# Two-layer hybrid attention trunk on one core: attention steps, weight splits and evictions put in another order inside the projection stages

## What is computed

```
h    = rmsnorm(x, norm_g)
proj = h @ w_in                      # 2048 -> 6400 columns: aq ak av ag bq bk bv bg
ya   = chunk_relbias_attention(...)  # mixer A: 16 heads of 64, own chunk + 8 before, bias by distance
ya   = ya * silu(ag)
yb   = swa_sink_gqa(...)             # mixer B: 16 query heads, 2 key heads, rotary, window 128, sinks
yb   = yb * silu(bg)
x    = x + concat([ya, yb]) @ w_out
```

## Time and profile before

| what | value |
|---|---|
| median of three executions | 1678.8 us |
| the profiled execution, its time | 1680.35 us |
| its span, first to last instruction | 1678.6 us |
| busy: PE, DVE, ACT, POOL | 96%, 76%, 56%, 23% |
| mean granted clock of PE | 0.994 |

### The profile page before, as it was taken

How to read it: one execution, slowest core, us unless ns; L and a number is a source line. 1 busy time by engine, 2 the same in 40 slices (tenths; PEclk the granted TensorE clock), 3 DMA queues, 4 the chain that set the end, 5 groups by cost and what they waited for, 6 DMA issues and landing times.

```text
span 1678.6 us, 28680 instructions
## 1 busy us (share of the span) xinstructions
PE 1613.9 (96%) x9257; PEld 1404.2 (84%) x9257; DVE 1279.6 (76%) x2747; ACT 935.3 (56%) x1969; POOL 386.4 (23%) x554
## 2 busy tenths in 40 slices
PE   8999999999999999999999999999999999999997
PEld 7888888888778888899987888888887888888997
DVE  7777777877677787888877777777776777788875
ACT  7656555565456665533465556655564566664333
POOL 1632332334022210000054332332321221000000
PEclk9999999999999999999999999999999999999999
DMA  6232333223422322344432322333324223233343
GB/s 229 79 94 76 98 97 101 87 81 95 158 91 90 103 97 91 109 157 153 158 112 72 104 90 80 96 94 99 94 80 162 88 93 115 76 113 107 129 142 113
DMA packets 77509, 180.67 MB, mean 108 GB/s; under 512 B 9408, under 2 KB 13792, under 8 KB 70640
## 3 DMA queue, kind: packets, MB, share of 16 engines
q1 hardware_dynamic: 76960, 178.99, 32.4%
q10 hardware_dynamic: 432, 0.55, 0.1%
q0 software_dynamic: 32, 0.08, 0.0%
HBM read 163.25 MB, written 11.62 MB: 104 GB/s over the span
## 4 chain that ended last, share of the span: by engine, by line
PE 48%; issue 29%; POOL 15%; DVE 4%; ACT 2%; POOLq 1%; DMA 0%; DVEq 0%; SPq 0%; ACTq 0%
PE ps_proj L711 9%; PE ps_proj L712 9%; PE ps_proj L713 9%; POOL w_raw L2251 4%; POOL w_raw L2253 3%; POOL w_raw L2256 3%; POOL w_raw L2254 3%; DVE w_lo L1553 1%; PE ps_o L993 1%; PE ps_o L997 1%; PE ps_o L998 1%; PE ps_o L823 1%; PE ps_s L798 1%; PE ps_s L982 1%; PE ps_s L981 1%
## 5 line engine op out<-in xcount | busy, mean ns | idle before, releaser
L1092 ACT ACTIVATE w_hi<-w_raw 128x512 fp32r<-128x512 f32 (+1 forms) x528 | 377.9, 726 | 234.2 <-DVE w_raw L1925 56.0
L1553 DVE TENSOR_TENSOR w_lo<-w_raw,w_hi 128x512 fp32r<-128x512 f32 (+1 forms) x528 | 442.3, 848 | 48.8 <-ACT w_hi L1092 45.4
L711 PE MATMUL ps_proj<-act_hi,w_hi 128*128 128x512 f32 x704 | 277.9, 395 | 0.0
L713 PE MATMUL ps_proj<-act_hi,w_lo 128*128 128x512 f32 x704 | 275.9, 392 | 0.0
L712 PE MATMUL ps_proj<-act_lo,w_hi 128*128 128x512 f32 x704 | 275.9, 392 | 0.0
L1553 DVE TENSOR_TENSOR arena<-ps_t,arena 128x512 fp32r<-128x512 f32 (+4 forms) x168 | 85.0, 509 | 130.1 <-ACT arena L1092 129.5
L2251 POOL TENSOR_TENSOR w_raw<-w_raw 128x128 f32<-128x128 f32 x112 | 65.0, 580 | 457.3 <-DMA w_raw<-w 457.3
L713 PEld LDWEIGHTS ps_proj<-act_hi,w_lo 128*128 128x128 f32 x704 | 132.8, 189 | 28.8
L711 PEld LDWEIGHTS ps_proj<-act_hi,w_hi 128*128 128x128 f32 x704 | 133.0, 189 | 25.0
L1158 ACT ACTIVATE probs<-probs,nmax 128x128 f32<-128x128 f32 (+3 forms) x128 | 72.0, 562 | 146.5 <-DVE nmax L1625 146.3
L712 PEld LDWEIGHTS ps_proj<-act_lo,w_hi 128*128 128x128 f32 x704 | 133.1, 189 | 24.4
(11 more groups left out here) (374 smaller groups left out, 4555.8 us busy)
## 6 DMA issues: line engine op xcount, KB each, us to landing
w_raw<-w SPq DMA_DIRECT2D x322, 256.0 KB, 3.0
w_raw<-w SPq DMA_DIRECT2D x51, 1024.0 KB, 4.9
temp<-temp SPq DMA_DIRECT2D x72, 64.0 KB, 4.2
strips_tables<-ext SPq DMA_DIRECT2D x16, 256.0 KB, 3.9
temp<-xT SPq DMA_DIRECT2D x16, 256.0 KB, 4.3
xs<-xy SPq DMA_DIRECT2D x16, 256.0 KB, 4.2
temp<-xs SPq DMA_DIRECT2D x16, 256.0 KB, 4.1
strips_tables<-ext SPq DMA_DIRECT2D x16, 224.0 KB, 4.1
```

Of the source, the lines that this page charges most:

```text
L711: pe.matmul(dst, wh, act_hi[:, k, :], start=start, stop=False)
L713: return pe.matmul(dst, wl, act_hi[:, k, :], start=False, stop=stop)
L1092: return nc.scalar.activation(dst, src, ACT.Copy, scale=scale)
L1553: return nc.vector.tensor_tensor(dst, src, hi, ALU.subtract)
```

## The change

Nothing is computed in another way; steps stand at other places. `values_a` goes from points 7 and 13 to 8 and 14, two points behind the last transposes it needs. ACT's `half_out` goes with it but stands last in its point, and DVE's `sum_halves` goes to points 12 and 15, with `gated` behind the second. ACT's normalising goes from the end of point p to the start of point p + 1. DVE does `lo_in` before `lo_p`, where it was after. DVE's splits of q and k for the next pair: k one point later (ACT's `hi_k` at 12, DVE's `lo_k` at 13). DVE's take of the second half, at a stage's end before, goes behind the first bias, low part and inversion of the next stage; stage 1 leaves it out. In the mixed stage PE no longer waits for a bank before the first two tiles.

```
-PV_A = (7, 13)
+PV_A = (8, 14)
+HALF_OUT_AT = (8, 14)
+SUM_HALVES_AT = (12, 15)
-HI_Q_AT, LO_Q_AT, HI_K_AT, LO_K_AT = 10, 11, 11, 12
+HI_Q_AT, LO_Q_AT, HI_K_AT, LO_K_AT = 10, 11, 12, 13
...
             def unit(T, att):
                 for s in range(4):
-                    wait_bank(T, s)
+                    if s > 1:
+                        wait_bank(T, s)
...
-            def softmax_a(e0, e, other):
-                n = (e % QT + 1) * P
-                row = probs[:, e % 2, 0:n]
+            def exp_a(e0, e):
+                row = probs[:, e % 2, 0:(e % QT + 1) * P]
...
-                other()
+            def normalise_a(e0, e):
+                row = probs[:, e % 2, 0:(e % QT + 1) * P]
                 act.wait_ge(rden_done, e0 + (e + 1))
                 copy(row, row, scale=rden[:, e % 2, 0:1]).then_inc(normed, 1)
...
+                if p - 1 in SCORES_A:
+                    normalise_a(e0, SCORES_A.index(p - 1))
                 if p in TURN_A:
                     hi_p(g, e0, TURN_A.index(p))
-                if p in PV_A:
-                    half_out(g, PV_A.index(p))
                 if p in SCORES_A:
-                    softmax_a(e0, SCORES_A.index(p), other)
-                else:
-                    other()
+                    exp_a(e0, SCORES_A.index(p))
+                other()
+                if p in HALF_OUT_AT:
+                    half_out(g, HALF_OUT_AT.index(p))
...
                 if p in SCORES_A:
                     bias_a(v, L * PAIRS + ab, e0, SCORES_A.index(p))
+                other()
                 if p in TURN_A:
                     lo_p(e0, TURN_A.index(p))
-                if p in PV_A:
-                    h = PV_A.index(p)
+                if p in SCORES_A:
+                    invert(e0, SCORES_A.index(p))
+                if p in SUM_HALVES_AT:
+                    h = SUM_HALVES_AT.index(p)
                     sum_halves(g, h, tile, (L * PAIRS + ab) * 2)
                     if h == 1:
                         gated(g, tile)
-                other()
-                if p in SCORES_A:
-                    invert(e0, SCORES_A.index(p))
...
                     attend(att, p, L, ab, Y_STAGE, other)
+                    if p == 0 and not first:
+                        take_pair(T - 4, L, u - 1, 1, ((t_graw, 0.5), (t_v, 1.0)))
...
-                take_pair(T, L, u, 1, ((t_graw, 0.5), (t_v, 1.0)))
...
                         attend(att, p, L, ab, ab, lambda: split_w(T, s + 1, pt))
+                        if p == 0:
+                            take_pair(T - 4, L, PAIRS - 1, 1, ((t_graw, 0.5), (t_v, 1.0)))
```

More of the change, by code:

```diff
@@ L1356, in duties @@
                 if kind == "b":
-                    if p == HI_K_AT:
+                    if p == 11:
                         hi_k(lambda: act.wait_ge(rope_done, L * ROPES + 1))
@@ L1770, in duties @@
                         take(T, 1, t_q)
-                    if p == LO_K_AT:
+                    if p == 12:
                         lo_k(L * V_LAYER + PAIRS)
@@ L1813, in take_pair, with unit_sums @@
                                                    ).then_inc(proj_free, 1)
-            def unit_sums(T, L, u, att, ab, g, v):
+            def unit_sums(T, L, u, att, ab, g, v, first=False, last=False):
                 for p in range(16):
                     def other():
-                        if isinstance(u, int) and p + LO_AHEAD >= 16:
+                        if last and p + LO_AHEAD >= 16:
                             lo_next(tile0(L) + A_SLOTS, p + LO_AHEAD - 16)
@@ L1822, in other @@
                             lo_in(T, p + LO_AHEAD)
-                    if p == PV_A[0]:
+                    if p == SUM_HALVES_AT[0]:
                         dve.wait_ge(y_kept, L * (16 * (PAIRS - 2)) + u * 16)
@@ L2103, in _ @@
                     carry_wait(dve)
-                with dve.Fori(1, PAIRS - 1) as u:
+                unit_sums(T + 4, L, 1, att_a(L, 0), 0, pair_a(L, 1), L * V_LAYER + 1, first=True)
+                with dve.Fori(2, PAIRS - 1) as u:
                     unit_sums(T + u * 4, L, u, att_a(L, u - 1), u - 1, pair_a(L, u), L * V_LAYER + u)
                 u = PAIRS - 1
-                unit_sums(T + u * 4, L, u, att_a(L, u - 1), u - 1, pair_a(L, u), L * V_LAYER + u)
+                unit_sums(T + u * 4, L, u, att_a(L, u - 1), u - 1, pair_a(L, u), L * V_LAYER + u, last=True)
                 unit(T + A_SLOTS, L, att_a(L, PAIRS - 1), PAIRS - 1, ("b", None, None))
```

## The result

The changed kernel takes 1699.17 us (median of four, 1698.0 to 1702.16) against 1678.13 (1676.68 to 1679.56) for the kernel before beside it: a ratio of 1.0128 with an interval of 1.0111 to 1.0146. It is slower; 1672 was predicted, and the range ended at 1691. The profiled execution took 1702.16 with a span of 1700.4, 21.8 more than before. The mean granted clock fell from 0.994 to 0.979.

A forecast was written before the change was run, and what follows sets the result against it. PE, busy 96% of the span, was taken as the bound, so only its waits could be won. 12 x 0.2 - 2 x 1.8 - 2 x 3.1 = -7.4 us gave 1672 us, range 1650 to 1691.

The forecast's parts named there:

- Waits that go: PE's waits before points 1, 10, 13 and 15 vanish in a middle stage; about 0.3 of 0.76 us stays at 12.
- `gated` at t = 1.3: DVE's 13.7 us of work ends `gated` 1.3 us after a stage's first score product (t = 0).
- L = 3.4: Landing time of chunk 4's load behind the store of y: 3.4 us, with bounds 3.0 and 4.7.
- third rival: Slower: load still lands after 4.7, wait 4.1 at point 3, half clock in every stage; 1693 us, chance 0.25.
- The rest of the chain: From chunk 4's landing to point 3 on PE: 2.86 + 1.99 us, plus 0.45 for the low part ahead of `lo_p` 0.
- The wait before point 3: PE waits for chunk 4's chain in stages 2 to 7: 2.8 us, against 0.65 before.
- Three in four of them at 1.65: Half clock behind the point 3 wait in three of four of stages 2 to 7: 1.2 us a stage.
- Stages 2 to 7, +0.2 each: Twelve stages each end 0.2 us longer: waits win 1.0, half clock costs 1.2.
- Stage 1: No store ahead of its chunk 4 in SP's list; small waits go, winning about 1.8 us, twice.
- The mixed stage, -3.1 each: Bank wait and half clock behind it go, less 0.4 at the first bias and 0.4 at point 3; 3.1 us won, twice.
- some 0.4 more at point 3 for the reordered `lo_p`: Mixed stage: low part now ahead of `lo_p` adds some 0.4 us of wait at point 3.
- Normalising costs nothing: ACT's normalising moved to the next point's start costs nothing of its own; uncovered it would be 0.5 to 0.7 us.

The follow-up runs named there:

- before_y_late: Kernel before the change, with the store of y moved behind the next stage's loads of chunks 4 and 5: 1677.07 us, ratio 0.9983.
- fill: Changed kernel with twelve unread 512-column products on PE before point 3 in stages 2 to 7: 1680.48 us, ratio 1.0014.
- take_end: Changed kernel with the second half's take back at the stage's end and the mixed stage's bank waits back: 1684.61 us, ratio 1.0025.
- y_late_mixed: y_late, and in the mixed stage the take behind the second bias and `lo_p` ahead of the low part: 1641.69 us, ratio 0.9779.
- norm_old: y_late_mixed with ACT's normalising back at the end of its point: 1641.61 us, ratio 0.9769.
- evict_old_alone: Changed kernel with values, `half_out` and `sum_halves` back at points 7 and 13, store of y not moved: 1671.41 us, ratio 0.9947.
- lo_p_first: Changed kernel with DVE's `lo_p` again ahead of the low part of the weights at every point: 1695.55 us, ratio 1.0096.
- ylm_lo_p_first: y_late_mixed with `lo_p` ahead of the low part of the weights in every stage: 1649.24 us, ratio 0.9821.
- y_late: Changed kernel with the store of y moved behind the next stage's loads of chunks 4 and 5: 1651.9 us, ratio 0.983.
- best: y_late_mixed with the take's scalings behind the second bias, and in the mixed stage the first bias earlier, pair 7's gating later: 1632.18 us, ratio 0.9715.
- evict_old: y_late_mixed with values, `half_out` and `sum_halves` back at points 7 and 13: 1664.5 us, ratio 0.9916.

## Why the prediction was wrong

The mechanism in stages 2 to 7 was right: the store behind a later `gated` holds chunk 4, the wait returns at point 3 with `lo_p` 0 at its end, and the clock falls. The sizes and the mixed stage were wrong, all the same way.

- *Waits that go.* The bias wait at point 1 in stages 2 to 7 and those before 10, 13 and 15 went. At point 12 0.42 stayed, 0.3 was said. Right.
- *`gated` at t = 1.3.* It ended at 2.15: DVE took 14.4 us for the work summed up as 13.7, and PE 12.1 where 12.3 was put. The k split was entered with its old 2.78, but it was moved one point later, beside POOL's sums of raw weights, and took 3.29; the low part behind it took 0.2 longer too. A duration of a moved step was carried to its new neighbours.
- *L = 3.4.* It was 3.4, for the reason given: the strips make the 4.7, as before_y_late shows. The term that the third rival turned on was right, and the rival's outcome came by another way.
- *The rest of the chain.* 2.86 + 1.99 + 0.45 was said, 2.85 + 2.54 came: 0.1 more.
- *The wait before point 3.* 3.49 in place of 2.8: 0.85 from `gated` and 0.1 from the chain, less 0.2 since PE itself could be there only at 8.78 and not 8.57. 0.7 x 12 = 8 us.
- *The clock.* "Three in four of them at 1.65" was 1.2 a stage. All twelve paid, 1.66 on average by fill, with half clock twice as long in stage 5: 0.45 x 12 = 5 us. I had made a chance out of one exception whose own wait, shorter now, paid this time (2.40 for 2.65). The rule of the Trainium skill, "TensorE: Matmul & The Clock Gate", section "HAM oscillation", that a wait repeated in each round throttles in each, held here in twelve of twelve waits of 3.3 us. For shorter ones it isn't a law: in take_end five of twelve waits of 2.3 us kept their clock, one in layer 0 and four in layer 1.
- *Stages 2 to 7, +0.2 each.* They gave 19.2 us in sum in place of 2.4, 1.6 each. Wait and clock by the two lines above make 1.15 a stage of the missing 1.4; the 0.1 at point 12 is another part. The last 0.15 may lie in the old waits, which I had from their idle times; no run here splits it further.
- *Stage 1.* -3.3 in place of -3.6. In layer 1 the clock fell in both kernels, and -2.5 came for -1.8; in layer 0 it fell only now, and -0.8 came. The sum is near by luck.
- *The mixed stage, -3.1 each.* It is the step that failed worst: +3.4 and +2.9, so 12.5 us for two. The bank wait went as said. But "some 0.4 more at point 3 for the reordered `lo_p`" was 2.66 of idle time, with half clock behind it, because I priced the new order of two steps and not the take of 2.4 us which the change put in front of the second bias; the exponential, ACT's high parts and `lo_p` 0 queue behind that bias. Moving it, with `lo_p` ahead of the low part, gave 10.2 us back (y_late_mixed). The first bias cost 1.15 and 1.00, not 0.4, as `gated` was late here too. And 1.59 of idle time stood before mixer B's value transposes, where 0.46 was before; no term of the sum had that wait.
- *Normalising costs nothing.* Right (norm_old).

The errors add up: 16.8 in the stages, 12.5 in the mixed ones, 0.3 in stage 1, -0.4 at the start make 29.2, the distance from the predicted -7.4 to the +21.8 of the profiled executions. Slower had 0.2, because I let only L decide that rival. Its own condition was a wait of 3.0 with half clock in every stage, and 2.8 stood 0.2 from it: an error of that size in DVE's sum of 13.7 was enough.

## What to carry to other kernels

When a step is made later, follow every queue that waits for its result: here one store of y, needed by nobody soon, stood ahead of loads on which all engines depend. The same late eviction cost 28 us with the store there and won 23 without. Order transfers by who needs them first, and ask of each long wait not only how long it is but whether another wait behind it will absorb the half clock that follows.

## What the runs showed of the chip

DVE and POOL slow each other when both read SBUF tensors. The forms of DVE's split of k, in the kernel before and after (count, busy us, mean ns):

```profile
L1553 DVE TENSOR_TENSOR k_st<-temp,k_st 64x512 fp32r<-64x512 f32 x72 | 50.4, 699 | 3.0 <-ACT k_st L1092 2.3
```

```profile
L1558 DVE TENSOR_TENSOR k_st<-temp,k_st 64x512 fp32r<-64x512 f32 x72 | 56.5, 785 | 3.0 <-ACT k_st L1095 2.3
```

And POOL's sums in the kernel after, beside that split and behind it:

```profile
218.22 0.91 POOL L2263 TENSOR_TENSOR w_raw<-w_raw 128x128 f32<-128x128 f32 x1
...
219.96 0.91 POOL L2260 TENSOR_TENSOR w_raw<-w_raw 128x128 f32<-128x128 f32 x1
220.95 0.46 POOL L2262 TENSOR_TENSOR w_raw<-w_raw 128x128 f32<-128x128 f32 x1
```

A sum takes 0.46 alone and up to 0.91 beside the split or beside the low part of the weights that follows it (219.96). In the kernel before, the split was over at 215.34 and POOL's sums began at 215.86. The Trainium skill says so in "SBUF — State Buffer", section "Who interferes with whom": a DVE instruction with two inputs in SBUF and a GpSimd instruction that reads SBUF contend for one port pair. The traces agree, and this would have warned of the 0.5 us that `gated` came late.

A load of 256 KB lands after 4.7 us right behind the strips and the store, after 3.4 behind the store alone, and after 3.0 in evict_old_alone, where the store had gone 4 us earlier. In before_y_late, with the strips right ahead and no store, it took 4.5. So the strips right ahead go with some 1.5 more, the store with at most 0.4.

Twelve products that nothing reads kept the clock at 1.00 over a wait in which it fell without them, at no cost while they fit in the wait. And with waits of the same length the time at half clock differed by a factor of two between stage 5 and the others, in both layers; why stage 5 has it stays open.

Nor does the length of a wait settle whether the clock falls. Half clock followed twelve of twelve waits of 3.3 us (the kernel after), eleven of twelve of 2.8 (lo_p_first), seven of twelve of 2.3 (take_end), none of four of 2.1 before point 1 of the mixed stage (lo_p_first, ylm_lo_p_first), and three of four of 2.0 at its start (the kernel before, before_y_late). The wait of 2.4 in layer 0's stage 1 was followed by it in the kernel after and in y_late. Waits of 2.38 to 2.43 at the same place weren't in y_late_mixed, best, evict_old and take_end.
